# Modulation by products and sums ahead of a gather, and two blocks' last units tile by tile

## Time and profile before

| | us |
|---|---|
| median of 3 runs | 2371.11 (2367.22 to 2376.46) |
| profiled execution | 2365.49 |
| its span, first to last instruction | 2363.7 |
| TensorE busy, share of the span | 1796.4 (76%) |
| VectorE | 1291.7 (55%) |
| ScalarE | 868.9 (37%) |
| GpSimd | 904.2 (38%) |
| mean granted TensorE clock | 0.83 |
| moved from HBM, gather loads of it | 681.40 MB, 536.90 MB |

### The profile page before, as it was taken

How to read it: one execution, slowest core, us unless ns; L and a number is a source line. 1 busy time by engine, 2 the same in 40 slices (tenths; PEclk the granted TensorE clock), 3 DMA queues, 4 the chain that set the end, 5 groups by cost and what they waited for, 6 DMA issues and landing times. The chain is left out here.

```text
span 2363.7 us, 25240 instructions
## 1 busy us (share of the span) xinstructions
PE 1796.4 (76%) x8848; PEld 1117.7 (47%) x8848; DVE 1291.7 (55%) x2801; ACT 868.9 (37%) x2355; POOL 904.2 (38%) x699
## 2 busy tenths in 40 slices
PE   8898899868777787564443468885377897999998
PEld 6775676445435255110000014331055676888786
DVE  4633668877787665656767676566403623333201
ACT  3122344333444343233643353333225734222212
POOL 1300334374663444344555544445400122444343
PEclk9999888777788889786555679986579998999999
DMA  6111999999999999999999999999953011122121
GB/s 246 54 63 49 403 410 392 418 377 411 411 401 418 418 418 417 417 404 406 419 420 420 419 405 419 418 397 419 420 178 110 1 72 71 72 107 107 72 107 54
DMA packets 108494, 687.78 MB, mean 291 GB/s; under 512 B 12240, under 2 KB 13264, under 8 KB 40144
## 3 DMA queue, kind: packets, MB, share of 16 engines
q0 software_dynamic: 73728, 536.90, 55.3%
q1 hardware_dynamic: 34640, 149.27, 16.9%
HBM read 681.40 MB, written 2.10 MB: 289 GB/s over the span
## 5 line engine op out<-in xcount | busy, mean ns | idle before, releaser
L747 PE MATMUL ps<-arena 128*32 128x512 f32 (+5 forms) x4376 | 872.7, 587 | 377.0 <-ACT arena L1452 337.3
L1696 POOL DMA_INDIRECT arena<-in_experts,arena_u x512 | 608.6, 1189 | 770.9 <-PE ps L747 678.2
L2001 DVE CUSTOM_DVE_ANT_0 arena<-arena 128x1024 f32<-128x1024 f32 x512 | 653.2, 1281 | 384.3 <-DMA arena<-in_experts,arena_u 367.5
L747 PEld LDWEIGHTS ps<-arena 128*128 128x128 f32 (+2 forms) x4376 | 443.2, 167 | 735.5 <-ACT arena L1452 496.6
L1448 ACT ACTIVATE sel<-sel 128x1 f32<-128x1 f32 x512 | 102.8, 201 | 705.4 <-DVE sel L2001 697.7
L1717 POOL TENSOR_TENSOR r_low<-middle,r_low 128x1024 fp32r<-128x1024 f32 x74 | 178.7, 2415 | 463.5 <-ACT r_low L1533 463.5
L747 PE MATMUL ps<-r_low 128*128 128x512 f32 x1248 | 286.4, 391 | 5.3 <-DVE r_low L2059 3.8
L747 PEld LDWEIGHTS ps<-r_low 128*128 128x128 f32 x1248 | 234.6, 189 | 56.8 <-DVE r_low L2059 4.4
L1452 ACT ACTIVATE arena<-arena,sel 128x32 f32<-128x32 f32 x512 | 164.5, 321 | 16.8 <-ACT sel L1448 0.2
L1533 ACT ACTIVATE r_low<-middle 128x1024 fp32r<-128x1024 f32 x74 | 78.3, 1058 | 208.1 <-PE ps L747 208.1
L747 PE MATMUL ps<-upper,arena 128*128 128x384 f32 (+5 forms) x640 | 144.9, 412 | 3.2 <-issue 3.0
(11 more groups left out here) (203 smaller groups left out, 1721.2 us busy)
## 6 DMA issues: line engine op xcount, KB each, us to landing
arena<-in_w_front SPq DMA_DIRECT2D x88, 512.0 KB, 3.5
middle<-in_w_late SPq DMA_DIRECT2D x18, 2048.0 KB, 8.2
arena<-in_w_qkv SPq DMA_DIRECT2D x48, 512.0 KB, 10.7
gtrow<-in_w_ada SPq DMA_DIRECT2D x32, 512.0 KB
arena<-in_experts,arena_u POOLq DMA_INDIRECT x512
arena<-in_w_ada SPq DMA_DIRECT2D x16, 512.0 KB, 10.0
x<-in_x SPq DMA_DIRECT2D x4, 512.0 KB, 8.7
arena<-in_sub_keys SPq DMA_DIRECT2D x2, 1024.0 KB, 10.4
```

Of the source, the lines that this page charges most:

```text
L747: return nc.tensor.matmul(out_, lhsT, rhs, start=start, stop=stop_, skip_group_check=skip)
L1696: nc.gpsimd.indirect_dma_start(ring[n % RING], None, a["experts"], bass.IndirectOffsetOnAxis(ap=idxq[:, i % 4, k:k + 1], axis=0),).then_in ...
L2001: nc.vector.tensor_tensor_reduce(r[:, 0:D], r[:, 0:D], xrep[k % 4], 1.0, 0.0, ALU.mult, ALU.add, dots[:, n % 8:n % 8 + 1]).then_inc(s["dot ...
```

## The change

**Modulation.** Another table, `w_mod`, holds the 4096 columns of shift and scale as rows: 32 tiles of 128x1024. `silu(c)` is also made as a row `crow`, the same on all partitions. For each tile SyncE loads 512 KB into one of the two halves of `gtrow`, GpSimd multiplies it by `crow` (`mod_product`), and ScalarE copies it with a running sum into one column of `modc` (`mod_sum`). They are placed by marks in the list of steps, all in the first half: `cv` 3 to 11, `mu` 1 and 3, six `u`, `s2` 0 and 1, `pm` 0 and 2, `wo` 0 to 7, `q` 1 to 6. At mark m, ahead of the step, SyncE issues load m (when sum m - 2 is done); behind the step, GpSimd makes product m - 1 and ScalarE sum m - 2. The matmuls of the modulation, their loads in the gather and L1505 are gone.

**Last units.** The last four units of O2 and of feed-forward out are no longer used one after the other: TensorE waits for all four and then works through them tile by tile (`split_last`). O2's four have buffers of their own, the very last two units of feed-forward out too. After O2 the transposes, shift and scale and splits are done by tile (`rows_after`, `low`), those of tile 0 ahead of the products of tile 3; VectorE takes half of the evacuations of tiles 2 and 3.

Cut to its core; the list of steps and the buffers:

```diff
+MARK_STAGES = [("cv", u) for u in range(3, QKV)] + [("mu", 1), ("mu", 3)] + [("u", (1, lv)) for lv in range(1, LEVELS)] \
+    + [("s2", 0), ("s2", 1), ("pm", 0), ("pm", 2)] + [("wo", k) for k in range(OUT_UNITS)] + [("q", j) for j in range(1, 7)]
...
-        mpair = gtrow[:, :, :].rearrange("p s (k n) -> p s k n", k=2)
+        crow = region(60, D)
...
         u_hi = [low3(32 + 8 * (u % 2), KD, P) for u in range(UNITS)]
         u_lo = [low3(36 + 8 * (u % 2), KD, P) for u in range(UNITS)]
+        for n, kb in enumerate((112, 120, 84, 92)):
+            u_hi[UNIT_O2 + 4 + n], u_lo[UNIT_O2 + 4 + n] = high3(kb, KD, P), high3(kb + 4, KD, P)
+        for n in range(2):
+            u_hi[UNITS - 2 + n], u_lo[UNITS - 2 + n] = low3(16 + 8 * n, KD, P), low3(20 + 8 * n, KD, P)
+        def split_after(u):
+            if UNIT_O2 + 4 <= u < UNIT_FIN:
+                return 0
+            if UNIT_FIN <= u < UNIT_FIN + 2:
+                return UNIT_O2 + 3 + u - UNIT_FIN
+            return UNIT_FOUT if u >= UNITS - 2 else u - 1
```

On SyncE:

```diff
+            def mod_rows(m):
+                if m is None or m >= MODS:
+                    return
+                if m < 2:
+                    sp.wait_ge(s["cs"], 1)
+                else:
+                    sp.wait_ge(s["mod"], m - 1)
+                sp.dma_start(gtrow[:, m % 2, :], a["w_mod"][m]).then_inc(m_pair[m % 2], 16)
...
+            sp.dma_start(crow, a["c_row"][0:1, :].broadcast_to([P, D])).then_inc(s["rows"], 16)
...
-            for at, h, stage, arg in STAGES:
-                done = mod_pairs(at, done)
+            for n_stage, (at, h, stage, arg) in enumerate(STAGES):
+                mod_rows(MARKS.get(n_stage))
```

On TensorE:

```diff
-            def modulation(k):
-                n, kd = k // 4, k % 4 * 2
-                pe.wait_ge(s["cs"], 1)
-                pe.wait_ge(m_pair[k % 2], 16 * (k // 2 + 1))
...
-                for lane in range(2):
-                    for j in range(4):
-                        ins = mm(ps[:, 5, 64 + 4 * n + j:65 + 4 * n + j], mpair[:, k % 2, lane, j * P:(j + 1) * P],
-                                 ccol[:, kd + lane:kd + lane + 1], kd + lane + j == 0, kd + lane == KD - 1, True)
-                ins.then_inc(s["mfree"], 1)
...
-                if k is not None and mod_load(k) == n:
-                    modulation(k)
...
+            def split_last(units, k_of, cols_hi, cols_lo, last, between):
+                for u in units:
+                    unit(u)
+                for t in range(T):
+                    for u in units:
+                        ins = split_tile_rows(t, u, k_of, cols_hi, cols_lo, last)
+                    if t < T - 1:
+                        ins.then_inc(s["y"], 1)
+                    between(t)
+                ins.then_inc(s["unit_used"], len(units))
...
-            pe.wait_ge(s["yfree"], T)
-            for t in range(T):
+            def rows_after(t):
+                pe.wait_ge(s["yfree"], t + 1)
                 pe.wait_ge(s["xs"], T + t + 1)
                 for kd in range(KD):
-                    ins = mm(ps[:, kd, t * P:(t + 1) * P], x[:, t, kd * P:(kd + 1) * P], tdiag[:, t, :])
+                    ins = mm(ps[:, 2 * t + kd // 4, kd % 4 * P:(kd % 4 + 1) * P], x[:, t, kd * P:(kd + 1) * P], tdiag[:, t, :])
...
+            split_rows(range(UNIT_O2, UNIT_O2 + 4), o_rows, a_hi, a_lo, KD - 1)
+            split_last(range(UNIT_O2 + 4, UNIT_FIN), o_rows, a_hi, a_lo, KD - 1, lambda t: rows_after(0) if t == 2 else None)
...
+            split_rows(range(UNIT_FOUT, UNITS - 4), fout_rows, act_hi, act_lo, FT - 1)
+            split_last(range(UNITS - 4, UNITS), fout_rows, act_hi, act_lo, FT - 1, lambda t: None)
```

On ScalarE:

```diff
+            def mod_sum(m):
+                if 0 <= m < MODS:
+                    sc.wait_ge(s["mprod"], m + 1)
+                    nc.scalar.activation(gtrow[:, m % 2, :], gtrow[:, m % 2, :], ACT.Copy, scale=0.5,
+                                         accum_out=flat(modc)[:, m:m + 1]).then_inc(s["mod"], 1)
...
                     front_stage(h, stage, arg)
+                    mod_sum(MARKS.get(n_stage, 0) - 2)
...
+            for t in range(3):
+                branch(0, t)
+                stats_after(t)
+            rows_after(0)
+            branch(0, 3)
+            rows_after(1)
+            stats_after(3)
             nc.scalar.preload_act_table_set("silu_and_others")
...
+            rows_after(2)
+            rows_after(3)
```

On GpSimd:

```diff
+            def mod_product(m):
+                if 0 <= m < MODS:
+                    pl.wait_ge(m_pair[m % 2], 16 * (m // 2 + 1))
+                    tt(gtrow[:, m % 2, :], gtrow[:, m % 2, :], crow, ALU.mult).then_inc(s["mprod"], 1)
...
                     front_stage(h, stage, arg)
+                    mod_product(MARKS.get(n_stage, 0) - 1)
```

On VectorE, and the new arrays:

```diff
-            for t in range(T + 1):
-                if t < T:
-                    branch(0, t)
-                if t >= 1:
-                    norm_after(t - 1)
+            for t in range(3):
+                branch(0, t)
+                norm_after(t)
+            low(0)
+            branch(0, 3)
+            rows_after(2)
+            norm_after(3)
+            low(1)
+            low(2)
+            rows_after(3)
+            low(3)
...
+        "w_mod": adaw[:, :4 * D].T.reshape(MODS, P, D), "c_row": g["c_2"][0][None, :],
```

More of the change, by code:

```diff
@@ L248, with marks @@
 STAGES = paced(front_plan(0) + front_plan(1))
+MARK_STAGES = [("cv", u) for u in range(3, QKV)] + [("mu", 1), ("mu", 3)] + [("u", (1, lv)) for lv in range(1, LEVELS)] \
+    + [("s2", 0), ("s2", 1), ("pm", 0), ("pm", 2)] + [("wo", k) for k in range(OUT_UNITS)] + [("q", j) for j in range(1, 7)]
+def marks():
+    out = {}
+    for n, (at, h, stage, arg) in enumerate(STAGES):
+        if at < 0 and (stage, arg) in MARK_STAGES:
+            out[n] = len(out)
+    return out
+MARKS = marks()
 LAG_ACT = {"tr0": 2, "cv": 1, "pz": 2, "tr1": 2, "q": 2, "sc": 2}
@@ L1122, in qkv_unit @@
                 ins.then_inc(s["used"], 1)
-            mods = iter(range(MODS))
-            k = next(mods)
             for n in range(LOADS):
@@ L1573, in _ @@
             nc.scalar.preload_act_table_set("sqrt_and_others")
-            for u in range(UNIT_O2 + 2, UNIT_FIN + 1):
+            for u in range(UNIT_O2 + 2, UNIT_FIN + 2):
                 split(u)
```

169 lines of the change are left out of this document (75 added, 94 removed).

## The result

| | before | changed |
|---|---|---|
| median of the runs | 2373.8 us (2367.2 to 2378.6) | 2398.8 us (2393.9 to 2401.6) |
| ratio | | 1.0115, 95% interval 1.0096 to 1.0135 |
| profiled execution, span | 2363.7 us | 2397.4 us |
| first gather load | 235.5 | 262.7 |
| first to last gather load | 1465.9 | 1464.3 |

A forecast was written before the change was run, and what follows sets the result against it. The gather was taken as bound by transfers from 262 us on; -32.5 + 12.5 + 6 + 9 - 2 + 6.5 = -0.5 us, so about 2370 us, no change, 8 in 10 range 2346 to 2391.

The forecast's parts named there:

- A: Gather: modulation transfers leave it, 38 us of queue time, for -32.5 us; bounds the whole 38, and 15.
- D: Start of the gather: product 29 behind eight gather loads holds ScalarE, load 8 comes 16.5 us late; +9 us.
- B: Convolution stage, first half: TensorE waits for GpSimd's matrices behind products, ScalarE's root stands behind a sum; +12.5 us.
- C: Output projection, first half: ScalarE runs four sums in a row ahead of the norm's square root; +6 us.
- E: End of the attention output: tile by tile gains 3.5 us, a lower clock takes back 1.5; -2 us.
- F: End of the last block: TensorE pauses 8.4 us, slower clock 2, chain behind it 3.9 shorter; +6.5 us.
- signs of being wrong: Front grows by under 8 us, the DMA dip is missing, or the gather keeps its length.
- the slower rival: The stretch 262 to 644 us is not bound by transfers, A saves 15 less 2.5; about 2390 us, chance 0.24.

The follow-up runs named there:

- e3: The kernel before with no modulation loads, matmuls, products or sums (bias alone), both ends as before; ratio 0.9893 to the kernel before.
- e6: The kernel before with one matmul instead of 16 for each pair of modulation weights, all transfers kept; ratio 0.9953 to the kernel before.
- e4: e1 with three more marks, so the last three products stand ahead of the first eight gather loads; ratio 1.0007 to the kernel before.
- e1: The modulation change alone, without the tile-by-tile ends of blocks; ratio 1.0089 to the kernel before.
- e7: e4 with each GpSimd product over 64 of its 1024 columns; ratio 0.9941 to the kernel before.
- e8: The kernel before with tile-by-tile ends alone, in the last block only for the last two units; ratio 0.9986 to the kernel before.
- e9: e4 with marks spread anew over the front, early products behind the matrices or masks TensorE needs; ratio 0.9931 to the kernel before.
- e2: The kernel before with the tile-by-tile ends of both blocks alone, modulation as before; ratio 1.0033 to the kernel before.

## Why the prediction was wrong

The sum was -0.5 us, and 27 were measured. No single step makes this miss: A, D and the front (B and C) were each put 7 to 10 us too low, E and F together 3.5. One of the signs of being wrong that I had named came true: the gather kept its length.

**A: -32.5 forecast, -25 measured** (e3's ratio, 19 to 32; -20 against the one trace of before). The size came near by luck; the mechanism, transfers that set the pace, failed. The transfers left as counted, but of their 38 us only 13 to 14 came back (e6 against e3), and TensorE's 74 us of matmuls, put at nothing because "it does not set the pace", were worth 11. The term of 3 us for what VectorE cannot follow should have been above 20. I compared busy time with the length of the stretch, 284 of 344 us, and called the rest slack. But 62 of VectorE's idle us before were other waits, most of them for other engines, in order with its dot products, and 52 of them are still there when transfers and matmuls are gone. Added up, busy and such waits make 383 of 423 us, and only 31 of the rest are waits for rows: 38 could never come back, and 31 only if all of them went. The lower bound that I gave (15) was worked out from just these waits; I had set it aside for a share of 1.00.

**D: +9 forecast, +17 measured** (e4 against e1). The mechanism was right, and its times within 2.5 us up to load 8; the size failed. Of the 16.5 us by which load 8 would be late I took 7.5 to be hidden behind full queues. It came 18.9 late and the gather lost 17. The queues ran empty 28 us behind the first load (at about 291 us), as counted, and lost 11 us up to load 8; some 5 us more were lost behind it, which my sum did not have.

**B and C: +18.5 forecast, +27.5 to +28.2 measured** (e1, e4 and the changed kernel, from the common step). The waits for the matrices were right (8.5 us of pause, where 9.5 us of delay were forecast). ScalarE's root in B cost 0.2 us, not 2.2. Missing were the lower clock behind each new pause (5.5 us) and most of the collisions (7.7 instead of 1.7); e7 puts both and the products' own length at 17.

**E: -2 forecast, +0.4 to +0.7 measured.** TensorE went on 1.2 us later than worked out, 2.3 us ahead of before instead of 3.5, and the clock of 0.67 over the next 8 us took 2.6 us of that back: nothing gained.

**F: +6.5 forecast, +7.5 measured**, with its three parts (8.3, 2.3 to 3, -3.7) as worked out, and e8 shows that the wait is the buffers of units 70 and 71.

The chances: the slower rival named the right mechanism, a stretch that is not bound by transfers, and the waits of the earlier trace rows together with VectorE's others should have given it more weight. That its 2390 us is nearest to 2399 is in part luck: its price of A, 15 less 2.5, lies further from the measured 25 than mine, and it had nothing for the matmuls; the rest of the measured time is D and the front, which it took over from the forecast.

What stays open: which of the order effects (SyncE's, GpSimd's or ScalarE's) makes up how much of D, since e4 moves all three; what the remaining 11 us at the front of e9 are; and why three gathers of the same instructions took 1466 to 1476 us.

## What to carry to other kernels

Before counting a transfer's time as gained, add to the consumer's busy time its waits for anything but that transfer: in an in-order engine they stay, and a DMA share of 1.00 does not exclude that they set the pace as soon as the queues are relieved. Work put into idle time costs by its place in each engine's order: the same 32 products and sums cost 28 us, 16 or 11 ahead of the gather, by a table of marks alone, and three of them behind a row of loads cost 17 more. For a pause of 3 to 5 us put in front of TensorE, add the slower clock behind it. And before two traces are set side by side, look at how far two executions of the same instructions differ, and count from a common step.

## What the hardware showed unexpectedly

Pauses of only 4 to 5 us, behind 30 and 10 us of steady matmuls, left TensorE at a mean granted clock of 0.75 and 0.67 for the next 7 to 8 us. In e7 the same two pauses were 1.95 and 2.98 us: behind the first the granted clock was 1.00, behind the second 0.79.

The start of the program differs from one execution to the next, with the same instructions: the same group of 32 matmuls of 256 columns took 9.86 us in the kernel before and 7.15 in e6. TensorE's timeline of the kernel before:

```profile
27.53 9.86 PE L747 MATMUL ps<-arena 128*128 128x256 f32 x32
```

and the same view of e6:

```profile
26.92 7.15 PE L747 MATMUL ps<-arena 128*128 128x256 f32 x32
```

The granted clock goes with it. From 24 to 34 us TensorE was busy without a pause in both (columns of the earlier trace rows; first the kernel before, then e6):

```profile
24.00:34.00 10.00, 10.00 (x46) 8.79 (x46) 3.04 (x14) 3.74 (x8) 1.04 (x1) 0.66 0.72 286
...
24.00:34.00 10.00, 10.00 (x62) 9.17 (x61) 5.46 (x19) 4.13 (x9) 1.04 (x1) 1.00 0.86 329
```

It was 0.66 in one and 1.00, full speed, in the other. So the first loads of two profiles can differ by 7 us with the same front (229.6 in e2, 236.9 in e8), and counted from a step behind the start by 1 us. What sets the clock there no run shows.

A pair of VectorE operations of 0.65 us each, against a row of GpSimd products with gaps of 0.3 us, takes as long as two products: 4.76 us. It fits a VectorE that gets one turn in each gap; no run here tests that alone.
